# Seven-product weights for five of the eight convolution iterations, with their sums on GpSimd

## The reference

```python
conv = causal_depthwise_conv(c_c * c_h, conv_w[layer])
y_b = (c_b * conv) * jax.nn.silu(c_g)
z_a = jnp.einsum('btc,cd->btd', y_a, w_branch_a[layer])
z_b = jnp.einsum('btc,cd->btd', y_b, w_branch_b[layer])
merged = (jax.nn.sigmoid(g_a + gate_bias[layer, 0]) * z_a
          + jax.nn.sigmoid(g_b + gate_bias[layer, 1]) * z_b)
```

## Time and profile before

| what | value |
|---|---|
| median of three runs | 2886.66 us |
| the profiled execution's own time | 2887.28 us |
| its span | 2885.6 us |
| matmuls on TensorE | 12935, busy 2849.9 us |
| VectorE busy | 1982.4 us |
| ScalarE busy | 1319.7 us |
| GpSimd busy | 6.7 us |
| DMA | 564.20 MB, 60.5% of 16 engines' span |

### The profile page before, as it was taken

One profiled execution on the slowest core, in us unless ns is written; L12 is line 12 of the kernel. 1 busy time (PEld: TensorE's weight loads), 2 busy tenths in 40 slices (PEclk: granted clock), 3 DMA queues, 4 the chain that ended last, 5 costly groups with the idle time before them and its releaser, 6 DMA issues.

```text
span 2885.6 us, 38782 instructions
## 1 busy us (share of the span) xinstructions
PE 2849.9 (99%) x12935; PEld 2357.6 (82%) x12935; DVE 1982.4 (69%) x2209; ACT 1319.7 (46%) x1420; POOL 6.7 (0%) x22
## 2 busy tenths in 40 slices
PE   8999999999999999999999999999999999999998
PEld 7888888888888788888887888888888888888776
DVE  6566766676667645555469686776868777886886
ACT  5443444344444444333445454454545445554554
POOL 0000000000000000000000000000000000000000
PEclk9999999999999999999999999999999999999999
DMA  7555555555555556655556666666666666766655
GB/s 236 184 178 168 173 176 175 169 173 179 175 170 175 187 192 193 191 190 189 189 182 204 199 221 200 212 209 204 214 200 218 199 214 206 240 202 215 213 203 204
DMA packets 416844, 564.20 MB, mean 196 GB/s; under 512 B 25745, under 2 KB 288002, under 8 KB 416770
## 3 DMA queue, kind: packets, MB, share of 16 engines
q1 hardware_dynamic: 416770, 563.25, 60.5%
HBM read 555.28 MB, written 7.86 MB: 195 GB/s over the span
## 4 chain that ended last, share of the span: by engine, by line
PE 94%; DVE 3%; DMA 1%; issue 1%; DVEq 1%; ACT 1%; SPq 0%; ACTq 0%
PE PS L1315 21%; PE PS L1317 21%; PE PS L1316 21%; PE QL L1442 7%; PE QL L1441 7%; PE QL L1440 7%; PE PS L1440 2%; PE PS L1442 2%; PE PS L1441 2%; PE QL L1346 2%; DMA RP<-in_w_out 1%; DVE QS L1079 1%; DVE QS L722 1%; DVEq L701 1%; PE QL L1323 0%
## 5 line engine op out<-in xcount | busy, mean ns | idle before, releaser
L722 DVE TENSOR_TENSOR QS<-RP,QS 128x1024 fp32r<-128x1024 f32 x716 | 872.7, 1224 | 732.2 <-ACT QS L444 715.8
L444 ACT ACTIVATE QS<-RP 128x1024 fp32r<-128x1024 f32 x716 | 755.8, 1059 | 1105.1 <-PE PS L1317 987.2
L1315 PE MATMUL PS<-QS,U 128*128 128x512 f32 x2176 | 860.2, 395 | 10.0 <-DVE QS L722 7.4
L1317 PE MATMUL PS<-QS,U 128*128 128x512 f32 x2176 | 849.4, 390 | 0.0
L1316 PE MATMUL PS<-QS,U 128*128 128x512 f32 x2176 | 848.6, 390 | 0.0
L1315 PEld LDWEIGHTS PS<-QS,U 128*128 128x128 f32 x2176 | 409.7, 188 | 96.1 <-issue 7.9
L1317 PEld LDWEIGHTS PS<-QS,U 128*128 128x128 f32 x2176 | 409.2, 188 | 86.8
L1316 PEld LDWEIGHTS PS<-QS,U 128*128 128x128 f32 x2176 | 409.9, 188 | 81.4
L1440 PE MATMUL QL<-QS,U 128*128 128x512 f32 x964 | 376.1, 390 | 3.3 <-DVE GA L1207 3.3
L1442 PE MATMUL QL<-QS,U 128*128 128x512 f32 x964 | 375.8, 390 | 0.0
L1441 PE MATMUL QL<-QS,U 128*128 128x512 f32 x964 | 375.7, 390 | 0.0
(11 more groups left out here) (252 smaller groups left out, 2127.3 us busy)
## 6 DMA issues: line engine op xcount, KB each, us to landing
RP<-in_w_in SPq DMA_DIRECT2D x1024, 256.0 KB
RP<-in_w_in SPq DMA_DIRECT2D x256, 512.0 KB
RP<-in_w_out SPq DMA_DIRECT2D x128, 512.0 KB
RP<-in_w_branch_a SPq DMA_DIRECT2D x64, 512.0 KB
RP<-in_w_branch_b SPq DMA_DIRECT2D x64, 512.0 KB
XS<-in_x SPq DMA_DIRECT2D x8, 512.0 KB, 5.5
XR<-in_x SPq DMA_DIRECT2D x16, 256.0 KB, 4.5
out_dram<-H SPq DMA_DIRECT2D x8, 512.0 KB, 3.9
```

What stands on the lines that cost most here:

```text
L444: act.activation(WS[s][:, :, 0:OW], RAW[s][:, :, :], ACT.Copy).then_inc(hi_ready, 1)
L722: dve.tensor_tensor(WS[s][:, :, OW:2 * OW], RAW[s][:, :, :], WS[s][:, :, 0:OW], ALU.subtract).then_inc(lo_ready, 1)
L1315: pe.matmul(bank, top, w[:, k, 0:OW], start=at_k == 0, stop=False)
L1317: op = pe.matmul(bank, low, w[:, k, 0:OW], start=False, stop=at_k == n_tiles - 1)
```

## The change

Convolution iterations 0 to 2 stay as they are. Iterations 3 to 7 are computed in the order of `GATES`, as 9 plain units and 7 sevens over all 1024 columns, with (b, g) as the first and (c, h) as the second group of 512. The sums of `U` are formed in iteration 2 instead of 7.

- GpSimd forms the four weight sums of each seven in these five iterations; VectorE's `seven` leaves them out there (`given=True`). In the merge and output stages VectorE forms them as before.
- SP loads each raw tile pair in two DMAs of 256 KB (as the convolution's loads were before). The first of them, for a slot that a seven used, waits for `t_sum`, since GpSimd's reads are not covered by `lo_ready`.
- At the end of an iteration ScalarE copies one bank of `PS` (`a_out`) and the four banks of `QL` (`front_out`, `back_out`) to `TX`, `GA` and `GB`, and VectorE adds the rest. TensorE's next product waits for these two before its first and its third quarter of unit 0.
- The two sigmoid gates become one sigmoid on ScalarE (`SIG`), and `CF`, `CSF`, `CSG`, `CK` are now parts of `GA` and `GB`.
- `turn_conv` of the iteration before goes in the middle of unit 1, into two banks of `PS`. ScalarE, not VectorE, copies them out (`CSF`, `UP`) after the first high part of the first seven's sums. `convolve` follows at units 3 and 5.

```diff
...
 GATE_BLOCKS = GATES.blocks - 1
+FIRST_SEVEN = 3
+CONVS = NP - FIRST_SEVEN
...
         GA, GB = [at(n, [P, 2, OW], region_g + i * 2 * OW * 4) for i, n in enumerate(("GA", "GB"))]
-        CF, CSG, CSF, CK = [at(n, [P, 2, T], region_g + 4 * W2 * i) for i, n in enumerate(("CF", "CSG", "CSF", "CK"))]
+        CF, CSF = GA[:, :, 0:T], GA[:, :, T:2 * T]
+        CSG, CK = GB[:, :, 0:T], GB[:, :, T:2 * T]
+        TX = at("TX", [P, 2, OW], region_y + (2 * KB - 2) * 2 * T * 4)
+        SIG = TX[:, 0, :].rearrange("p (b c) -> p b c", b=2)
...
-            with sp.Fori(0, NP) as i:
+            with sp.Fori(0, FIRST_SEVEN) as i:
                 branch(i, (BLOCK_BG, BLOCK_CH), CONV_CHUNK)
+
+            def load_conv(i, k, c, chunk, sum_done):
+
+                s = c % RING
+                src = w_in[0][k * P:(k + 1) * P, 0:8 * BW].rearrange("p (g c) -> p g c", c=BW)
+                for g, blocks in enumerate((BLOCK_BG, BLOCK_CH)):
+                    if g == 0 and sum_done is not None:
+                        sp.wait_ge(t_sum, sum_done)
+                    if g == 1 or sum_done is None:
+                        sp.wait_ge(lo_ready, chunk - (RING - 1))
+                    dst = RAW[s][:, g, :].rearrange("p (a c) -> p a c", a=2)
+                    sp.dma_start(dst, src[:, blocks, bass.ds((i + 1) * GW - GW, GW)]).then_inc(raw_loaded[s], 16)
+
+            def conv_seven(i, first=False):
+
+                chunk, sums = CONV_CHUNK + BRANCH * i, sums_at(i - FIRST_SEVEN)
+                n_th = 0
+                for u, (kind, j) in enumerate(GATES.units):
+                    sum_done = sums - 1 if u == 0 and not first else None
+                    if u >= 2 and GATES.units[u - 2][0] == "S":
+                        n_th += 1
+                        sum_done = sums + (2 * n_th - 1)
+                    for h in range(2):
+                        load_conv(i, j + KH * h, 2 * u + h, chunk + 2 * u + h, None if sum_done is None else sum_done + h)
+
+            conv_seven(FIRST_SEVEN, first=True)
+            with sp.Fori(FIRST_SEVEN + 1, NP) as i:
+                conv_seven(i)
...
                 for u, (_, j) in enumerate(GATES.units):
+                    if first and u == 0:
+                        sp.wait_ge(t_sum, sums_at(CONVS))
...
+            def weight_sums(i, u, n_th):
+
+                chunk, n = CONV_CHUNK + BRANCH * i + 2 * u, GATES.first[u]
+                s = 2 * u % RING
+                w12, w11, w22, w21 = [RP[s // 2][:, q, :] for q in range(4)]
+                sums = [QF[:, (n + 3 + q) % QRING, OW:2 * OW] for q in range(4)]
+                for t in (s, s + 1):
+                    pool.wait_ge(raw_loaded[t], (chunk - s) * (16 * KC // RING) + 16 * KC)
+                for q, (x, y) in enumerate(((w11, w12), (w22, w12), (sums[0], w22), (sums[2], w21))):
+                    pool.wait_ge(block_used, used_at(i - FIRST_SEVEN) + (n + 3 + q - QRING + 1))
+                    op = pool.tensor_tensor(sums[q], x, y, ALU.add)
+                    if q >= 2:
+                        op.then_inc(t_sum, 1)
+                    if q in (1, 2):
+                        pool.drain()
+
+            def conv_seven(i):
+
+                n_th = 0
+                for u, (kind, _) in enumerate(GATES.units):
+                    if kind == "S":
+                        weight_sums(i, u, n_th)
+                        n_th += 1
+
+            pool.wait_ge(v_ready, 1)
+            conv_seven(FIRST_SEVEN)
+            with pool.Fori(FIRST_SEVEN + 1, NP) as i:
+                conv_seven(i)
...
                 branch(i, 0, a=i - 1)
             branch(0, CONV_CHUNK, a=NP - 1, is_conv=True, scaled=True)
             branch(1, CONV_CHUNK, is_conv=True, norm=True)
-            with act.Fori(2, NP - 1) as i:
-                branch(i, CONV_CHUNK, is_conv=True)
-            branch(NP - 1, CONV_CHUNK, is_conv=True, last=True)
...
                     op.then_inc(t_hi, 1)
+                    if conv_of is not None and m == 0:
+                        act.wait_ge(conv_turned, conv_of + 1)
+                        act.activation(CSF[:, :, :], pair(PS[0][:, 0, :]), ACT.Copy)
+                        act.activation(UP[:, :, 2:T + 2], pair(PS[0][:, 1, :]), ACT.Copy).then_inc(conv_read, 1)
...
+            def conv_seven(i):
+                chunk, used = CONV_CHUNK + BRANCH * i, used_at(i - FIRST_SEVEN)
+                product_hi(GATES, chunk, used, sums_at(i - FIRST_SEVEN), conv_of=i - 1)
+                act.wait_ge(block_used, used + (GATES.first[GATES.last_seven] + 6))
+                act.wait_ge(y_ready, i + NP)
+                act.activation(TX[:, 1, :], PS[0][:, 0, :], ACT.Copy).then_inc(a_out, 1)
+                for c in range(RING):
+                    if c == 2:
+                        act.wait_ge(front_done, i + (1 - FIRST_SEVEN))
+                        act.activation(GA[:, :, :], QL[:, 0:2, :], ACT.Copy).then_inc(front_out, 1)
+                    if c == 3:
+                        act.wait_ge(w_used, chunk + 2 * CD)
+                        act.activation(GB[:, :, :], QL[:, 2:4, :], ACT.Copy).then_inc(back_out, 1)
+                    next_hi(GATES, chunk, used, c)
+                act.wait_ge(front_summed, i + (1 - FIRST_SEVEN))
+                act.activation(SIG, CSF[:, :, :], ACT.Sigmoid).then_inc(gate_sig, 1)
+
+            act.wait_ge(v_ready, 1)
+            conv_seven(FIRST_SEVEN)
+            with act.Fori(FIRST_SEVEN + 1, NP) as i:
+                conv_seven(i)
...
-            def convolve(a, step, factor, u, held=False):
+            def convolve(a, step, factor=None, u=None):
 
                 if step == 0:
                     dve.wait_ge(conv_turned, a + 1)
                     dve.memset(UP[:, :, 0:2], 0.0)
-                    op = dve.tensor_copy(UP[:, :, 2:T + 2], pair(u))
-                    if held:
-                        op = dve.tensor_copy(CSF[:, :, :], pair(factor))
-                    op.then_inc(conv_read, 1)
+                    dve.tensor_copy(UP[:, :, 2:T + 2], pair(u)).then_inc(conv_read, 1)
                     after()
                 if step == 1:
+                    if u is None:
+                        dve.wait_ge(conv_read, a + 1)
                     for j in range(3):
                         for t in range(2):
                             tap = VT2[:, bass.ds(a * 2 + (16 * j + t), 1)]
...
@@ -1052,28 +1149,27 @@
                 branch(i, 0, a=i - 1)
             branch(0, CONV_CHUNK, a=NP - 1, is_conv=True)
             branch(1, CONV_CHUNK, is_conv=True, conv_of=0, norm=True)
-            with dve.Fori(2, NP - 1) as i:
-                branch(i, CONV_CHUNK, is_conv=True, conv_of=i - 1, unscaled=True)
-            branch(NP - 1, CONV_CHUNK, is_conv=True, conv_of=NP - 2, unscaled=True, last=True)
-
-            def seven(plan, chunk0, used, sums_at, u, n_th):
+            branch(2, CONV_CHUNK, is_conv=True, conv_of=1, unscaled=True, last=True)
+
+            def seven(plan, chunk0, used, sums_at, u, n_th, given=False):
...
-                w12, w11, w22, w21 = [RP[s // 2][:, q, :] for q in range(4)]
-                sums = [QF[:, (n + 3 + q) % QRING, OW:2 * OW] for q in range(4)]
...
+            def conv_seven(i):
+                chunk, used, sums = CONV_CHUNK + BRANCH * i, used_at(i - FIRST_SEVEN), sums_at(i - FIRST_SEVEN)
+                n_th = 0
+                for u, (kind, _) in enumerate(GATES.units):
+                    if u < AHEAD_UNITS:
+                        continue
+                    if kind == "S":
+                        seven(GATES, chunk, used, sums, u, n_th, given=True)
+                        n_th += 1
+                    else:
+                        for h in range(2):
+                            plain(GATES, chunk, u, h)
+                    if u in (3, 5):
+                        convolve(i - 1, (u - 1) // 2)
+                a, c, d, e = PS[0][:, 0, :], PS[0][:, 1, :], PS[1][:, 0, :], PS[1][:, 1, :]
+                dve.wait_ge(a_out, i + (1 - FIRST_SEVEN))
+                dve.tensor_tensor(TX[:, 0, :], c, TX[:, 1, :], ALU.add)
+                after()
+                dve.tensor_tensor(TX[:, 1, :], d, TX[:, 0, :], ALU.add)
+                for n in range(2):
+                    lo(chunk + 2 * CD + n, n)
+                after()
+                dve.wait_ge(front_out, i + (1 - FIRST_SEVEN))
+                dve.tensor_tensor(GA[:, :, :], GA[:, :, :], TX[:, :, :], ALU.subtract)
+                after()
+                for b in range(2):
+                    op = dve.tensor_tensor(GA[:, b, :], e, GA[:, b, :], ALU.add)
+                op.then_inc(front_summed, 1)
+                lo(chunk + 2 * CD + 2, 2)
+                dve.wait_ge(back_out, i + (1 - FIRST_SEVEN))
+                dve.tensor_tensor(GB[:, 0, :], a, GB[:, 0, :], ALU.add)
+                dve.tensor_tensor(GB[:, 1, :], GB[:, 1, :], TX[:, 1, :], ALU.add).then_inc(drained, 1)
+                after()
+                lo(chunk + 2 * CD + 3, 3)
```

(100 more changed lines are left out.)

38 lines of the change are left out of this document (19 added, 19 removed).

## The result

The kernel after takes 2911.14 us (median of 4 runs, 2910.09 to 2913.57), the kernel before 2886.47 us on the same chip (4 runs, 2885.54 to 2888.61). The ratio is 1.0086 with a 95% interval of 1.0068 to 1.0103: 25 us slower, where 2866 us was forecast and 2907 was the upper end of the range. The profiled execution took 2910.32 us, with a span of 2908.3.

What follows compares the result with a forecast made beforehand. TensorE, busy 99%, was taken as the bound: execution 2887.28 - 23.8 (fewer matmuls) + 2.5 (seams) = 2866.0, median 2865.4, rounded up to 2866 us. Range of this case 2862 to 2872; 8 in 10, 2861 to 2907.

Steps and rivals of the forecast that it cites:

- The count: TensorE, five converted iterations: 384 to 363 matmuls each, 105 fewer in all at 0.227 us, 23.8 us less.
- GpSimd's sums: Each seven: four adds and two drains on GpSimd take 4.6 us of 10.21, deadline met with 3.7 us over.
- rival A: VectorE and GpSimd take turns on SBUF: pairs of 11.5 us against 10.21, 40 us in all, 2906 us; chance 0.30.
- Add: One 512-wide add on GpSimd: 1.1 us taken, between 0.52 and 1.4.
- Seam: Between two products: VectorE done at E+7.4, TensorE's transposes at E+8.2 (E: end of the first product), margin 0.8 us.
- 0.5 us an iteration: Allowance for seams between products in the five converted iterations, 2.5 us in all.
- Raw slots: Landing, sums 4.6 and reload 5.35 us make 9.95 against a period of 10.21: fits by 0.26 us.

Runs made afterwards that it cites:

- E5: E1 with the two `convolve` steps cut into six pieces, one behind each of units 3, 5, 7, 9, 11 and 13: 2863.44 us, ratio 0.9924.
- E3: E1 plus five GpSimd multiplications of a 384-column tile beside each seven, which no engine waits for: 2939.98 us, ratio 1.0191.
- E2: The kernel after with each GpSimd add replaced by a drain and two memsets that read nothing, waits and signals kept: 2865.82 us, ratio 0.9932.
- E1: The kernel after with the weight sums of the five iterations back on VectorE and GpSimd idle: 2875.74 us, ratio 0.9968.
- E4: The kernel after with the DMAs of each unit's second raw tile bringing 128 of 256 columns per slice: 2911.96 us, ratio 1.0091.

## Why the prediction was wrong

The count held: 12935 to 12830 matmuls, 23.8 us. Where nothing is in the way it is paid almost in full: E5 is 22.6 us faster than before.

The step that failed is **GpSimd's sums**. It asked whether GpSimd could do four adds in its 10.21 us and meet its deadline, as if VectorE's work and GpSimd's lay side by side. They lie one behind the other. VectorE's two-input operations of a pair (6.3 us) and four adds of 1.28 (5.1) are 11.4 us; 11.3 was measured. Taking 2.7 us from VectorE put 5.1 into the same line. That the sum comes so close is in part luck: an add holds VectorE up for about 1.1 of its 1.28 us, and the 0.2 us between adds are not in the sum (E3 shows the sum too high, 13.2 against 11.7). The forecast for the kernel without this effect, 2866 us, is what E2 gives, 2865.8.

The effect was rival A, with the right mechanism, nearly the right pair (11.5) and time (2906), and it had a chance of 0.30. Its 11.5 was lucky: the adds were counted 0.7 us too short, and 0.8 us of handovers stood beside them that the measured pair leaves no room for. The sentence "even with VectorE's sums gone, the two together fill the pair" stood there. The weight against it was only that the trace of before could not show it, which is no evidence either way. This is the rule of the Trainium skill (SBUF — State Buffer, "Who interferes with whom") quoted in the prediction, that the one that starts first keeps the shared read interface to its end; the traces agree: 1.6 us of the 1.75-us low product lie behind the add's end, and memsets, which don't read, held up none of VectorE's two-input operations in E2.

The smaller terms:
- *Add.* 1.1 us was taken, with 1.4 as the upper end; it is 1.28. The Trainium skill's scaled estimate (GPSIMD Engine Reference, 3.1) of 1.1 to 1.2 was also low. The operations alone come to 11.4, and 11.3 was measured.
- *Seam.* The margin of 0.8 us was worked out rightly: E1 and E2 have no stall there. It was used up by the same cause, 3.1 us over three products. Its restart at the low clock was not foreseen.
- *0.5 us an iteration.* In E1 the loss is 3.3 us (86.5 against 83.2), and it comes from a place that the forecast did not price: the two `convolve` steps, 3.0 and 2.5 us in pairs with 1.2 us to spare. The 4.4 us of these operations stood in the prediction, but only under rival A. In E2, where VectorE is free of the sums, its waits cost TensorE 1.9 us over more than four iterations, so the omission did not move the forecast. In E5, where they fit, the loss is 0.4 us an iteration.
- *Raw slots.* They had room. From the last add's end to the next landing was 4.2 us (SP's issues 0.8, the transfer 3.4), not 5.35, since half of the bytes go earlier; E4 shows no gain from less.

## What to carry to other kernels

Work that reads SBUF on GpSimd is not free capacity beside VectorE: add both engines' reading time over a period and compare the sum with the period of the engine that bounds the kernel. The sum is a rough upper figure (11.4 for a measured 11.3, 13.2 for 11.7), but it says where to look. Before moving work off an engine, see how much it has to spare in the tightest period and whether its lumps can be cut to fit: here six small pieces in place of two gave more than the second engine could. And if a mechanism's arithmetic fills the period, "the trace cannot show it" is no reason to bet against it.
